# Dilated attention: queries and keys turned by VectorE in 32x32 squares that DMAs carry to their partitions, instead of by TensorE

## The reference, cut to what matters

```
q_b = apply_rope(rms(heads(aq)) * qn, cos, sin)
k_b = apply_rope(rms(heads(ak)) * kn, cos, sin)
for g, (window, dilation) in enumerate(((128, 1), (512, 4), (2048, 16))):
    o_g, lse_g = dilated_window_attention(q_b[g], k_b[g], v_b[g], window, dilation)
```

## Time and profile before

| | |
|---|---|
| median of the runs | 2664.25 us |
| the profiled execution's own time | 2663.26 us |
| its span, first to last instruction | 2661.5 us |
| TensorE busy | 2655.3 us, 100% of the span |
| VectorE busy | 1955.0 us, 73% |
| ScalarE busy | 1427.5 us, 54% |
| GpSimd busy | 174.1 us, 7% |
| bytes moved by DMA | 482.97 MB, mean 181 GB/s |
| matmuls of the units, line L368, 128x512, w_high with xT_parts | 2304, mean 395 ns |

### The profile page before, as it was taken

One profiled execution on the slowest core, in us unless ns is written; L12 is line 12 of the kernel. 1 busy time (PEld: TensorE's weight loads), 2 busy tenths in 40 slices (PEclk: granted clock), 3 DMA queues, 4 the chain that ended last, 5 costly groups with the idle time before them and its releaser, 6 DMA issues.

```text
span 2661.5 us, 42258 instructions
## 1 busy us (share of the span) xinstructions
PE 2655.3 (100%) x15756; PEld 2250.4 (85%) x15756; DVE 1955.0 (73%) x2650; ACT 1427.5 (54%) x2021; POOL 174.1 (7%) x98
## 2 busy tenths in 40 slices
PE   9999999999999999999999999999999999999999
PEld 8888888888888888888888888888888888888888
DVE  6776767777776876777776788567777768886676
ACT  5446565445446565544545667554454466765543
POOL 0000000000000000000000232000000013210000
PEclk9999999999999999999999999999999999999999
DMA  7555455656565445556555554546555655454553
GB/s 238 189 175 191 150 170 168 200 189 198 189 201 189 147 160 182 176 190 194 182 190 187 199 166 162 182 154 205 191 179 190 210 180 172 160 189 159 185 191 130
DMA packets 317212, 482.97 MB, mean 181 GB/s; under 512 B 16288, under 2 KB 196896, under 8 KB 317088
## 3 DMA queue, kind: packets, MB, share of 16 engines
q1 hardware_dynamic: 316800, 481.18, 55.3%
q10 hardware_dynamic: 288, 0.07, 0.0%
HBM read 478.02 MB, written 1.05 MB: 180 GB/s over the span
## 4 chain that ended last, share of the span: by engine, by line
PE 99%; DVE 0%; ACT 0%; issue 0%; DVEq 0%
PE bank L368 53%; PE bank L570 22%; PE bank L568 11%; PE bank L473 5%; PE bank L921 2%; PE bank L959 1%; PE bank L387 1%; PE bank L1611 0%; PE bank L951 0%; PE bank L1142 0%; PE bank L1099 0%; PE bank L1092 0%; PE bank L930 0%; PE bank L1591 0%; PE bank L1670 0%; PE bank L934 0%
## 5 line engine op out<-in xcount | busy, mean ns | idle before, releaser
L330 DVE TENSOR_TENSOR w_low<-raw,w_high 128x2048 fp32r<-128x2048 f32 x435 | 1005.3, 2312 | 413.3 <-ACT w_high L325 412.8
L325 ACT ACTIVATE w_high<-raw 128x2048 fp32r<-128x2048 f32 x435 | 831.0, 1912 | 482.6 <-PE bank L568 242.9
L368 PE MATMUL bank<-w_high,xT_parts 128*128 128x512 f32 x2304 | 742.1, 395 | 0.0
L570 PE MATMUL bank<-xT_parts,w_high 128*128 128x512 f32 x2560 | 618.6, 391 | 0.0
L570 PEld LDWEIGHTS bank<-xT_parts,w_high 128*128 128x128 f32 x2560 | 472.1, 188 | 92.1
L368 PEld LDWEIGHTS bank<-w_high,xT_parts 128*128 128x128 f32 x2304 | 432.6, 188 | 89.5
L368 PE MATMUL bank<-w_low,xT_parts 128*128 128x512 f32 x1152 | 448.7, 390 | 0.0
L568 PEld LDWEIGHTS bank<-xT_parts,w_low 128*128 128x128 f32 x2560 | 334.5, 191 | 16.7
L568 PE MATMUL bank<-xT_parts,w_low 128*128 128x256 f32 x2560 | 339.4, 282 | 0.0
L665 ACT ACTIVATE siluT<-gateT 128x256 f32<-128x256 f32 x160 | 66.9, 418 | 407.6 <-DVE gateT L721 407.1
L368 PEld LDWEIGHTS bank<-w_low,xT_parts 128*128 128x128 f32 x1152 | 216.6, 188 | 42.4
(11 more groups left out here) (308 smaller groups left out, 2706.5 us busy)
## 6 DMA issues: line engine op xcount, KB each, us to landing
raw<-in_w_in SPq DMA_DIRECT2D x288, 512.0 KB, 4.6
raw<-in_ffn_w_in SPq DMA_DIRECT2D x176, 512.0 KB, 4.5
raw<-in_ffn_wd SPq DMA_DIRECT2D x88, 512.0 KB, 4.1
raw<-in_ffn_w_out SPq DMA_DIRECT2D x88, 512.0 KB, 4.2
raw<-in_ffn_wg SPq DMA_DIRECT2D x86, 512.0 KB, 3.8
raw<-in_ffn_wu SPq DMA_DIRECT2D x86, 512.0 KB, 4.7
raw<-in_w_out SPq DMA_DIRECT2D x32, 512.0 KB, 4.3
raw<-in_w_branch_a SPq DMA_DIRECT2D x16, 512.0 KB, 4.8
```

The lines of the kernel that those rows point to most:

```text
L325: nc.scalar.activation(wh[slot][:], raw[slot][:], ACT.Copy).then_inc(high_done[slot], 1)
L330: nc.vector.tensor_tensor(wl[slot][:], raw[slot][:], wh[slot][:].bitcast(F32), ALU.subtract).then_inc(low_done[slot], 1)
L368: mm = pe.matmul(o[:, 0:n], x[:, rows], w[slot][:, col + j * n:col + (j + 1) * n], start=start and first, stop=stop and last)
L570: mm = pe.matmul(bank[:], wh[s][:, w], xhl[:, kt, :, :], start=kt == 0, stop=False, skip_group_check=True)
```

## The change

TensorE's turns of the six parts, their waits, and ScalarE's two copies out of PSUM go. In their place, in the same step of VectorE as the rotation, four `transpose` instructions turn the part in squares of 32x32, each 128 partitions by 256 elements, into a new tile `asq` (4 KB for each partition, at the place of `rope_sq`). SP then sends four DMAs of 128 KB from it to a second tile `aland` (at the place of `o_b`), each from 32 partitions to 128. ScalarE makes one copy of 128x1024 from there to `aqT` or `akT`. The partitions of the result are in another order than before, the same for queries and keys. SP's DMAs stand in step 29 + 2a, ahead of the load of unit 29 + 2a; they wait for the squares and for ScalarE's copy of the part before. VectorE waits before the rotation of part a for the landing of part a - 1, since `asq` shares its place with `rope_sq`. SP's wait at step 41 and ScalarE's moves into `stg` now wait for the squares.

```diff
-LINKS = {1: 58, 2: 30}
+LINKS = {1: 58, 2: 36}
...
+        asq = over("a_squares", [P, 1024], 74)
+        aland = over("a_turned", [P, 4, 4, TT, 32], 12)
...
+        def squares_home(sp, src, dst, landed):
+
+            for a in range(4):
+                sp.dma_start(dst[:, a].rearrange("p h t j -> p (h t j)"),
+                             src[a * 32:(a + 1) * 32, :].rearrange("i (b x) -> i b x", b=4)).then_inc(landed, 16)
...
-        NSEC = 4 + 6
+        NSEC = 4
...
+                a, odd = divmod(u - AQ0 - 7, 2)
+                if odd == 0 and 0 <= a < 6:
+                    sp.wait_ge(asq_turned, at2(lay, 6, a + 1))
+                    if a > 0:
+                        sp.wait_ge(sec_out2, at2(lay, 6, a))
+                    squares_home(sp, asq, aland, aT_in)
                 if u == 41:
                     sp.wait_ge(chunk_out2, at2(lay, CH2, max(AV_CHUNKS) + 1))
-                    sp.wait_ge(sec_T2, at2(lay, NSEC, NSEC))
+                    sp.wait_ge(asq_turned, at2(lay, 6, 6))
...
-            a, odd = divmod(u - AQ0 - 3, 2)
-            if odd == 0 and 0 <= a < 6:
-                pe.wait_ge(rope_done2, at2(lay, 6, a + 1))
-                if a == 0:
-                    pe.wait_ge(oh_out, at2(lay, 2, 1))
-                else:
-                    pe.wait_ge(sec_out2, at2(lay, 6, a))
-                for i in range(2):
-                    tr = turn_tokens(pe, wk[2 + i], stg[a % 2], 2 * i)
-                tr.then_inc(sec_T2, 1)
...
-                        act.wait_ge(sec_T2, at2(lay, NSEC, 4 + c - AQ_CHUNK - 1))
+                        if c - AQ_CHUNK >= 2:
+                            act.wait_ge(asq_turned, at2(lay, 6, c - AQ_CHUNK - 1))
                         dst = stg[(c - AQ_CHUNK) % 2]
...
-                    act.wait_ge(sec_T2, at2(lay, NSEC, 4 + a + 1))
-                    for i in range(2):
-                        dst = (aqT, akT)[a // 3][:, 4 * (a % 3) + 2 * i:4 * (a % 3) + 2 * i + 2, :]
-                        if a == ATT_GROUPS:
-                            r = nc.scalar.activation(dst, wk[2 + i][:].rearrange("p (k n) -> p k n", k=2), ACT.Copy)
-                        else:
-                            r = nc.scalar.activation(dst.rearrange("p h (t c i) -> p (h t) c i", t=TT, c=4), by_residue(wk[2 + i]), ACT.Copy)
+                    act.wait_ge(aT_in, at2(lay, 384, 64 * (a + 1)))
+                    dst = (aqT, akT)[a // 3][:, 4 * (a % 3):4 * (a % 3) + 4, :]
+                    if a == ATT_GROUPS:
+                        r = nc.scalar.activation(dst.rearrange("p h (t k j) -> p (h t) k j", t=TT, k=4), aland[:].rearrange("p k h t j -> p (h t) k j"), ACT.Copy)
+                    else:
+                        r = nc.scalar.activation(dst.rearrange("p h (t c k i) -> p (h t c) k i", t=TT, c=4, k=4),
+                                                 aland[:].rearrange("p k h t (c i) -> p (h t c) k i", c=4), ACT.Copy)
                     r.then_inc(sec_out2, 1)
...
+                    if a > 0:
+                        dve.wait_ge(aT_in, at2(lay, 384, 64 * a))
                     nc.vector.tensor_tensor(r8[:, :, :, 0:H], x[:, :, :, H:DH], sin[:, :, :, 0:H], ALU.mult)
                     nc.vector.tensor_tensor(r8[:, :, :, H:DH], x[:, :, :, 0:H], sin[:, :, :, H:DH], ALU.mult)
                     link(dve, nc.vector.tensor_tensor(rsq[:].rearrange("p t (h d) -> p t h d", d=DH), x, cos, ALU.mult))
-                    nc.vector.tensor_tensor(stg[a % 2][:], rsq[:], rtm[:], ALU.add).then_inc(rope_done2, 1)
+                    link(dve, nc.vector.tensor_tensor(stg[a % 2][:], rsq[:], rtm[:], ALU.add))
+                    for b in range(4):
+                        to = asq[:, b * SEQ:(b + 1) * SEQ]
+                        if a != ATT_GROUPS:
+                            to = to.rearrange("p (x c i) -> p x i c", c=4, i=8)
+                        r = nc.vector.transpose(to, x[:, :, :, b * 32:(b + 1) * 32].rearrange("p t h j -> p h t j"))
+                    r.then_inc(asq_turned, 1)
```

More of the change, by code:

```diff
@@ L309, in build @@
         merged2 = sem("merged2"); oaT_done = sem("oaT_done"); oaTh_done = sem("oaTh_done"); oaTl_done = sem("oaTl_done"); obT_done = sem("obT_done")
-        obTh_done = sem("obTh_done"); obTl_done = sem("obTl_done"); ob_out = sem("ob_out"); proj_out2 = sem("proj_out2"); rope_done2 = sem("rope_done2")
+        obTh_done = sem("obTh_done"); obTl_done = sem("obTl_done"); ob_out = sem("ob_out"); proj_out2 = sem("proj_out2"); asq_turned = sem("a_squares_turned"); aT_in = sem("a_turned_in")
         rsr_in = sem("rstd_residues_in"); vres_in = sem("a_v_residues_in")
@@ L1475, in unit2_done @@
             eng.wait_ge(slot_used[slot_of(u)], use(2, slot_of(u), lay, mix_use(u) + 1))
-        def by_residue(bank):
-            return bank[:].rearrange("p (k i c) -> p k c i", k=4, c=4)
         def by_token(bank):
```

## The result

The changed kernel takes 2673.31 us (median of 7 runs, 2672.63 to 2675.53), the kernel before 2664.11 us beside it: ratio 1.0037, 95% interval 1.0028 to 1.0046, 9.2 us slower. The forecast was 2668.6: the right sign, and a little under half the size. The profiled execution took 2672.75 us, with a span of 2671.0.

What follows compares the result with a forecast made beforehand. TensorE, busy 100%, and VectorE's queue near unit 32 were taken as two bounds at once. Two layers add 4.3 us to the profiled 2663.26, giving 2667.6; plus 1.0 for the median, 2668.6 us, range 2662 to 2680.

Steps and rivals of the forecast that it cites:

- TensorE's gain: Twelve turns of eight transposes leave TensorE: 10.4 us over two layers, if all of it reached the end.
- The chain and its places: VectorE's splits hold TensorE at units 32, 34 and 36 of each layer: 4.1 us idle at 32, 1.6 at 34.
- This chain starts 0.80 earlier: Before unit 31's split on VectorE: TensorE reaches the release 0.80 us earlier, one turn being gone, so the chain does too.
- T: VectorE's added cost for each part: four transposes at 0.35 us plus a 0.10 link, 1.5 us; bounds 0.9 and 2.5.
- 2.17: Microseconds by which each layer was forecast to be longer, at unit 36's start: 3T - 2.33.
- DMAs at no cost: Four DMAs for each part, last square landing 5.3 us after SP can send; cover and air hide them, cost nothing.
- The clock: Rival: TensorE's idle time lowers its clock to 1.2 GHz; one unit adds 5 us (2673), two give 2684; chance 0.06.
- Half rate: Rival: VectorE transposes at twice the time for each element, T = 2.5, 15 us slower, 2679 us; chance 0.12.
- Hidden after all: Rival: VectorE has unseen slack, so TensorE's 10.4 us come out in full, 2653.8 us; decides under T = 0.78; chance 0.10.

## Why the prediction was right or wrong

- **The number.** 2673.31 us lie in the wide range of 2662 to 2680, but outside the 2667.7 to 2671 that the forecast gave for its own mechanism. The mechanism held; two terms of it were too small, the next bullets say which.
- **TensorE's gain.** Right in what it said would become of it: all of it went into waits for VectorE (15.5 us in two layers) and the slow clock behind them.
- **The chain and its places.** Right: units 32, 34 and 36, released by the split. The first pause was put at 4.1 us and was 3.93, but from 1645.1 to 1649.1 and not from 1643.3 to 1647.4: its two ends came 1.8 and 1.7 us later, so its length fitted although its place did not. At unit 34 it was 0.32 instead of 1.6, since the slow clock had used it up.
- **"This chain starts 0.80 earlier".** This step failed. It started 0.9 to 1.0 us later. I looked for air before the splits of units 29 and 31 and did not ask who waits for the other instructions behind part 0's squares. The cross copy ended just before TensorE wanted it, so nearly all of part 0's T became a wait of TensorE at unit 25, and that release is the head of the chain. In all the head came 1.8 us a layer later than forecast. The run with the cross copy first divides this: 1.3 us go with the wait, and 0.5 stay, since three scattered parts (6.1 us) use up the air that VectorE had ahead of unit 31 (6.25 us idle before, less the 0.80 of an earlier head), which three parts at the forecast 1.5 would not have done. The prediction named what would show it, no idle time of TensorE anywhere but at units 32, 34 and 36; at unit 25 that did not hold.
- **T = 1.5.** Right for plain squares (1.45), too small for scattered ones (2.03), which are five of six parts. Parts 4 and 5 stand in the chain behind its head: 1.1 us a layer. The price was in the range's bounds (0.9 to 2.5), not in the sum; the sum took it from other instructions of the same size, none of them with writes known to be scattered.
- **The sum of both.** 2.17 + 1.8 + 1.1 = 5.1 us at unit 36, against 4.9 measured.
- **DMAs at no cost.** Right. Landing took 2.6 us where 3.5 was taken, and leaving the DMAs out changed nothing beyond the interval. The late loads did show up as waits of ScalarE, also without effect.
- **The clock.** The rival's condition came true. Its price did not in the changed kernel: the drop lasted less than one unit, and TensorE still waited 1.90 us at unit 36 behind it. Where less cover was left, the price was paid: 1.6 us behind unit 36 with the cross copy first, about 0.9 a layer without squares, 1.6 in one layer with the keys by TensorE. So the times of these runs hold some slow clock beside the chain, and the chain's own terms are read from the starts of units. The Trainium skill's statement (TensorE: Matmul & The Clock Gate, Part 1) that an idle engine is set back to 1.2 GHz agrees with the clock of 0.50 behind the pause.
- **Half rate.** Refuted: 0.34 us for 128x256 in plain order. The Trainium skill (Vector Engine (DVE) Microarchitecture Reference, 3.8 The reshape front-end and per-opcode configuration) gives one element per cycle per lane for a transpose. The plain ones bear that out as far as rows can, since they come at the pace of the products of the same size (0.34 against 0.33 us); the scattered ones, at 0.49, do not.
- **Hidden after all.** Refuted by the waits. Even without squares, where T was 0.22 and so under the rival's 0.78, only 2 us of the 10 were gained.

How much of the 1.8 us at the head and of the 1.1 us of scattering each gives in the final time is known from ratios only to about 3 us (half the width of an interval); the timelines carry the split. When a pause brings the clock down and when it does not stays open: at unit 36 a pause of 1.90 us left it full in the changed kernel, and one of 1.87 brought it down with the cross copy first.

## What to carry to other kernels

When work moves from a full engine to one with a low average load, read the other engine's timeline in exactly the stage where the work lands, and for each instruction queued behind it ask who waits for it and with how much slack; the copy nobody thought of cost 1.3 us of the 4.9 a layer here. Give the new work to the parts of the stage where the engine has air, and move what is not yet due out of the full window: half of the change, with one copy put first and two products put later, was faster than both kernels. Count a pause of TensorE for more than its length: the slow clock behind one cost up to 1.8 us, and it is hidden only where TensorE waits again further on. An idle GpSimd is no free place for elementwise work beside a busy VectorE.

## What the runs showed of the hardware that was not expected

- A VectorE transpose of 128x256 in float32 is issued every 0.34 us when it writes in order and every 0.49 us when consecutive elements go to places 8 elements apart; an addition of 128x1024 with writes 4 elements apart took 1.84 us to the next instruction instead of 1.15.
- Beside two GpSimd products of 128x1024, eight VectorE instructions of 128x128 took 6.50 us instead of 2.19.
- Around a pause of 3.93 us TensorE's granted clock fell from 1.00 to 0.50, and it was full again within 5 us of the pause's end. It also fell behind shorter pauses, of 2.73 and 2.57 us, and behind one of 1.87 but not behind one of 1.90.
